# Expert weights: the down weights go to ScalarE's DMA queue, the gate-up weights stay on the sync engine's

## The reference

```
g_sel = argmax(group logits)                     # 4 groups
top_v, top_i = top_k(expert logits in group, 2)  # 8 experts in a group
eid = g_sel * 8 + top_i                          # 2048 (token, expert) pairs, 32 experts
def expert_block(xb, e):
    gu = xb @ w_gate_up[e]                       # (rows, 1024) @ (1024, 1024)
    return (silu(gu[:, :512]) * gu[:, 512:]) @ w_down[e]   # (rows, 512) @ (512, 1024)
y[token] += gate * expert_block(...)
```

## Time and profile before

| | us |
|---|---|
| median of 3 runs | 2285.24 (2283.81 to 2295.14) |
| the profiled execution's own time | 2287.18 |
| its span, first to last instruction | 2285.3 |
| expert stage of layer 0, first gather to last block (about) | 600 to 1160 |
| expert stage of layer 1 | 1682 to 2242 |

### The profile page before, as it was taken

How to read it: one execution, slowest core, us unless ns; L and a number is a source line. 1 busy time by engine, 2 the same in 40 slices (tenths; PEclk the granted TensorE clock), 3 DMA queues, 4 the chain that set the end, 5 groups by cost and what they waited for, 6 DMA issues and landing times. The chain is left out here.

```text
span 2285.3 us, 47659 instructions
## 1 busy us (share of the span) xinstructions
PE 1986.2 (87%) x20952; PEld 1196.2 (52%) x20952; DVE 919.7 (40%) x1928; ACT 420.0 (18%) x963; POOL 407.0 (18%) x513
## 2 busy tenths in 40 slices
PE   6899999997598888888969999998958978898893
PEld 4777666666355454545545444444635545455561
DVE  2555555553621111111137998994261111111114
ACT  2332233223210000000123111222321000011010
POOL 2111111111121212222222000000112222222220
PEclk9999999999698989999989999998969999999997
DMA  8000000003599989899957221200359998989985
GB/s 317 1 1 1 1 0 0 0 1 140 200 425 402 393 365 389 366 384 423 411 187 200 57 61 50 56 0 0 160 203 427 406 392 361 393 368 406 421 367 229
DMA packets 96889, 512.23 MB, mean 224 GB/s; under 512 B 22790, under 2 KB 56634, under 8 KB 80304
## 3 DMA queue, kind: packets, MB, share of 16 engines
q1 hardware_dynamic: 74328, 463.00, 49.9%
q0 software_dynamic: 19456, 37.82, 4.9%
q10 hardware_dynamic: 2904, 8.44, 0.9%
HBM read 496.56 MB, written 34.65 MB: 232 GB/s over the span
## 5 line engine op out<-in xcount | busy, mean ns | idle before, releaser
L1249 PE MATMUL ps<-wgu,xT 128*32 128x256 f32 x10752 | 641.6, 393 | 2.2 <-DVE xT L1392 2.2
L1249 PEld LDWEIGHTS ps<-wgu,xT 128*32 128x32 f32 x10752 | 344.3, 114 | 264.5 <-issue 45.3
L1399 DVE TENSOR_TENSOR hh<-sg,ps 128x128 f32<-128x128 f32 x168 | 65.9, 393 | 663.8 <-ACT sg L1083 663.5
L1264 PE MATMUL ps<-wd,hhT 128*32 128x256 f32 x5376 | 319.9, 379 | 0.0
L1144 POOL DMA_INDIRECT y_rows<-my,yidx x168 | 166.8, 993 | 831.3 <-ACT my L1077 809.0
L1835 DVE SCALAR_TENSOR_TENSOR acc<-u,par,acc 128x512 f32<-128x512 f32 x400 | 268.4, 746 | 0.0
L1264 PEld LDWEIGHTS ps<-wd,hhT 128*32 128x32 f32 x5376 | 170.0, 110 | 120.1
L1231 PE MATMUL ps<-ident,xg 128*128 128x128 f32 x512 | 88.3, 328 | 134.3 <-DMA xg<-h_rows,hidx 134.3
L1083 ACT ACTIVATE sg<-ps 128x128 f32<-128x128 f32 x168 | 46.6, 277 | 782.7 <-PE ps L1249 782.7
L1392 DVE TENSOR_TENSOR xT<-ps,g_exp 128x384 f32<-128x384 f32 (+2 forms) x128 | 59.0, 502 | 247.1 <-PE ps L1231 247.1
L1231 PEld LDWEIGHTS ps<-ident,xg 128*128 128x128 f32 x512 | 69.7, 167 | 161.7 <-DMA xg<-h_rows,hidx 136.6
(11 more groups left out here) (307 smaller groups left out, 1746.0 us busy)
## 6 DMA issues: line engine op xcount, KB each, us to landing
wgu<-in_moe_w_gate_up SPq DMA_DIRECT2D x64, 4096.0 KB, 17.5
wd<-in_moe_w_down SPq DMA_DIRECT2D x64, 2048.0 KB, 16.8
w_in_sb<-in_w_in SPq DMA_DIRECT2D x4, 2048.0 KB, 14.2
h_rows<-wgu ACTq DMA_DIRECT2D x16, 512.0 KB, 12.3
wg<-in_conv_w_pw SPq DMA_DIRECT2D x16, 512.0 KB, 4.1
wa<-in_conv_w_pw SPq DMA_DIRECT2D x16, 512.0 KB, 5.5
wgu<-y_rows SPq DMA_DIRECT2D x16, 512.0 KB, 9.8
w_out_sb<-in_w_out SPq DMA_DIRECT2D x1, 4096.0 KB, 29.3
```

The costliest lines, as they stand in the source:

```text
L1249: mm = pe.matmul(ps[TB * g:TB * g + TB, GU + n % 2, 0:2 * P].rearrange("p (a f) -> p a f", a=2), xT[:, q % 2, j, TB * tl:TB * tl + TB], wg ...
L1264: mm = pe.matmul(ps[TB * g:TB * g + TB, Y + n % 2, 0:D // 4], hhT[:, n % 2, TB * j:TB * j + TB], wd[:, q % 3, j, D // 4 * g:D // 4 * g + D ...
```

## The change

The sync engine's loop issues only the gate-up loads. The down loads are issued by ScalarE, inside its loop over the blocks: after the result of the last block of place q has been copied to `my`, ScalarE reads the expert number of place q+3 from `order` and issues its down load. The load for place 2 is issued at n = 3, directly ahead of that for place 3. The waits for the routing stand there too. Sizes, buffers and the number of loads stay as they were. `load_down` is the same function, called with `act` in place of `sp`.

```diff
                     sp.wait_ge(gu_done, last_of[q - 3] + 1)
                 load_gate_up(sp, e, q % 3)
-                if q > 2:
-                    sp.wait_ge(d_done, last_of[q - 3] + 1)
-                load_down(sp, e, q % 3)
...
                 if n >= 1:
                     y_evacuate(n - 1)
+                if n == 3:
+                    act.wait_ge(order_ready, 1)
+                    act.wait_ge(over_ready, 1)
+                    for m in range(4):
+                        act.wait_ge(h_stored[m], 16 * NT // 4)
+                    load_down(act, act.value_load(order[0:1, 2:3], min_val=0, max_val=NE - 1), 2)
+                q, tl = blocks_of[n - 1]
+                if n >= 1 and n - 1 == last_of[q] and q + 3 < NE:
+                    load_down(act, act.value_load(order[0:1, q + 3:q + 4], min_val=0, max_val=NE - 1), q % 3)
             y_evacuate(NB - 1)
```

## The result

| | before | after |
|---|---|---|
| median | 2284.52 us (4 runs, 2283.52 to 2295.14) | 2520.41 us (4 runs, 2518.7 to 2520.58) |
| ratio | | 1.1019, 95% interval 1.0986 to 1.1052 |
| span of the profiled execution | 2285.3 us | 2516.9 us |

The account below looks back on a forecast made before the run. TensorE was taken to wait for small gathers beside the weights, not for bandwidth or weights. 2287.2 + 197.5 (short-cover gathers) + 16.6 (first gathers) = 2501.3, less 1.9 for the median: 2500 us, range 2335 to 2570.

Parts of the forecast that it names:

- One packet of each queue in turn: DMA engines alternate packets between queues whatever their size; with three, a POOL turn costs 1.14 + 0.57 = 1.71 us.
- The first rival: POOL's queue gets a turn after every weight packet of either queue: 0.86 us a turn, 18 us in all, 2303; chance 0.09.
- The second: Rival: nothing changes, as all weights in flight must move anyway and order doesn't matter to the gather; 2285 us, chance 0.06.
- the third: Rival: gathers wait for bytes queued ahead in the weights' queue, a third of which moves away; 84 us faster, 2201, chance 0.05.
- The fourth: Rival: ScalarE is late, its 4.22 us of cover gone, gathers unchanged; 51 us slower, 2336, chance 0.07.
- ScalarE's group of instructions: Register load, companions and DMA issue per down load on ScalarE: 60 of about 0.85 us, hidden, taken as 0 (bound 51 us).
- The term that counts: With two weight queues each short-cover gather takes 19.9 us in place of 12.0: 7.9 later, 25 times, 197.5 us.
- short-cover gather: The gather of each pair issued at the start of a place with only two blocks; TensorE waits for it, landing 14.34 us.
- ten dear turns: Turns of POOL's queue beside both gate-up and down packets during one short-cover gather: ten at 1.71 us, the other 4.9 at 0.57.
- The count: Waits of TensorE for a short-cover gather: 13 in layer 0 and 12 in layer 1, 25 together.
- The first gathers: Gathers at each layer's start: 7.9 us later less slacks of 2.4 and 5.1, so 8.3 us per layer, 16.6 in all.
- The weights: The pair's second gate-up load lands about 1926 instead of 1925.3, wanted two places later: covered; a few us at layer start.

Follow-up runs that it names:

- the one-queue run: Against the kernel before: from place 3 on ScalarE issues both gate-up and down loads, all in its one queue; 2301.14 us, ratio 1.0039.

## Why the prediction was right, point by point

*What bounds the kernel.* Right: taking the wait for gathers away by an earlier gather gave 3.7%. Of the 134 us, the 45.7 ahead of the gate-up matmuls took the place, with the DMA engines always busy.

*One packet of each queue in turn.* Right, also for three queues (62, 62, 63). The first rival, a turn for POOL after each weight packet, would have shown 124. The second, no change, and the third, faster, fell by the result and by the halved loads. The fourth, ScalarE's cover, fell by the one-queue run.

*ScalarE's group of instructions*, 0.85 us expected. The rows of the kernel after:

```profile
L1091 ACTq TENSOR_LOAD <-order x29: 279/284/312, 1826.9 to 2442.7; - x29
L1091 ACTq FUSED_REGOPS  x29: 147/147/153, 1827.2 to 2443.0; - x29
...
L996 ACTq DMA_DIRECT2D wd<-in_moe_w_down x30: 339/339/349, 1826.5 to 2443.4; - x30
```

With three small ones of 18, 51 and 29 ns about 0.87 us, and it lies where it was put, in the idle time between copy and silu:

```profile
2058.64 0.38 ACT L1074 ACTIVATE my<-ps 128x256 f32<-128x256 f32 x1 [1.45 <-PE ps L1270]
2059.32 0.34 ACTq L996 DMA_DIRECT2D wd<-in_moe_w_down  x1
2063.25 0.28 ACT L1080 ACTIVATE sg<-ps 128x128 f32<-128x128 f32 x1 [4.22 <-PE ps L1255]
```

*The term that counts*, 7.9 us for each short-cover gather: in the pair shown it is 22.12 - 14.34 = 7.8. Over all it was too small. In layer 1 the waits outside the first places were 61.6 us in 12, 5.1 each, and are 165.3 in 12, 13.8 each: 8.6 more. The gather after the change was sized well: 14.34 + 7.9 makes 22.2, and the twelve took 22.4 on average (21.8 to 23.3). What was off is the gather before. The twelve took 11.9 to 16.2 us, 13.7 on average, and the pair from which the term was worked out was one of the slower ones; I had used the working of one pair for all. Two of the last three, where no overflow DMA stands ahead of the gather, took only 12.5 and 11.9. The first nine waits rose by 8.4 us on average (from 5.7 to 14.2), the last three by 9.2 (from 3.4 to 12.6). The second of these last, before and after:

```profile
2126.52 1.09 PE L1231 MATMUL ps<-ident,xg 128*128 128x128 f32 x8 [2.42 <-DMA xg<-h_rows,hidx]
```

```profile
2347.63 1.97 PE L1237 MATMUL ps<-ident,xg 128*128 128x128 f32 x8 [12.37 <-DMA xg<-h_rows,hidx]
```

*How the ten dear turns came out.* The total of the pair was met better than its parts. From 2064 to 2068, and from 2080 to 2084:

```profile
q10 hardware_dynamic: 67, 1.10, 64.0%
q1 hardware_dynamic: 33, 0.56, 32.5%
q0 software_dynamic: 82, 0.09, 6.7%
...
q10 hardware_dynamic: 78, 1.23, 73.0%
q1 hardware_dynamic: 21, 0.16, 9.7%
q0 software_dynamic: 79, 0.13, 8.6%
```

In these two stretches q0 had 5.1 and 4.9 turns, at 0.8 us each. In the 12 us between them it moved 108 packets, 6.75 turns at 1.78 us. Together that is 16.8 turns in 20 us, where the sum had 14.9 in 19.9, ten of them dear. Fewer turns were dear, since two of q1's ten turns in that time were the small packets that end a load: its 161 packets carried 4.23 MB, which is 129 of 33 KB. The sum had counted such a packet like one of weights. Why q0 moved two turns more than before, no run shows. The two errors cancel, so that the pair came out at 7.8 us is in part luck.

*The count*, 25 gathers: one too many. The 13 of layer 0 in the earlier trace rows include the very first gather of the stage, which waits with no weights beside it. There were 24 such waits. In layer 0 they rose from 63.5 to 164.2 us in 12, 8.4 each, in layer 1 by 103.7: together 204.4 us where the sum had 197.5.

*The first gathers*, 5.5 + 2.8 us per layer: place 3 waits 9.2 us in either layer (18.5 in all, the sum had 16.6) and place 4 not at all, since the wait for place 3 gives it the cover:

```profile
1851.43 1.97 PE L1237 MATMUL ps<-ident,xg 128*128 128x128 f32 x8 [9.22 <-DMA xg<-h_rows,hidx]
```

*The weights.* Gate-up B took 20.3 us to land (forecast about 18, before 17.5) and down A 19.2 (before 12.1); nothing waited for either. q10 carried 134.27 MB, as forecast.

*What the sum lacked* was the growth of TensorE's busy time, 8.7 us. The turns' 6.1 of it follow from the clock behind longer waits. The gate-up group's 5.3 (641.6 to 646.9) are not shown to: the one-queue run by ScalarE has 647.3 with waits for gathers as short as before. With 204.4 + 18.5 + 8.7 = 231.6 the terms account for the span's growth; the forecast had 214.

## What to carry to other kernels

Ask of a small, latency-bound transfer what one of its packets waits for: here a packet of every other queue that had work, whatever its size. The second queue for bulk loads added no bandwidth, as the engines were near full already (429 GB/s from 2068 to 2075 with three queues; with two, from 1908 to 1920 before, 4.88 + 0.34 MB in 12 us is 435), and it made each of those turns dearer. Keep bulk loads in one queue, or cut them so that their packets are smaller. Better still, issue the small transfer as early as its buffer allows: the earlier gather was worth 3.7% here, somewhat more than the best layout of the weights (3.2%, halved gate-up loads in one queue).

## What the runs showed of the hardware that was not expected

The packet of a weight load is as long as the run of bytes that it fills on a partition: 33 KB for whole gate-up loads, 16 KB for down loads. With halved gate-up loads in one queue the packets became shorter with it. From 1900 to 2000:

```profile
DMA packets 4466, 41.88 MB, mean 419 GB/s; under 512 B 1365, under 2 KB 1369, under 8 KB 2087
...
q1 hardware_dynamic: 2660, 38.72, 91.7%
```

The 4466 - 2087 = 2379 packets over 8 KB carry nearly all of the 38.72 MB, 16 KB each.

Smaller packets cost bandwidth, but little: with the DMA engines always busy, 424 GB/s with packets of 33 and 16 KB and 406 with 4 KB. (The loads of 4 KB packets are also more and smaller DMAs; no run separates the two.) Halved loads in one queue, again over the middle of layer 1:

```profile
1700.00:2140.00 440.00, 402.88 (x6920) 239.79 (x6912) 73.35 (x192) 46.06 (x140) 112.79 (x112) 0.98 1.01 421
```

An indirect DMA whose 128 rows are all out of bounds, as those of the overflow table are with these inputs, is not free: it moved 32 packets (1024 fewer in the run without these 32 DMAs).

What is left open is how much of the 82 us that the second queue still costs with the earlier gather lies with the scatters and how much with the gathers; the run meant for it took away too few turns to tell.
